# Experts of a mixture layer: the array's two column halves take two column sets of one 128-row piece, transposes turn, row halves scatter

## The reference, cut to what matters

```python
def moe_ffn(h, w_router, b_router, w_gu, b_gu, w_down, b_down):
    logits = h @ w_router + b_router
    top_logit, top_idx = lax.top_k(logits, 4)        # 4 of 32 experts
    top_p = softmax(top_logit)
    ...
    def expert_block(tok, p, e):                     # tok: the tokens of expert e
        gu = h_pad[tok] @ w_gu[e] + b_gu[e]          # 1024 -> 2048
        glu = minimum(gu[:, :1024], 7.0)
        lin = clip(gu[:, 1024:], -7.0, 7.0)
        act = glu * sigmoid(1.702 * glu) * (lin + 1.0)
        return (act @ w_down[e] + b_down[e]) * p     # 1024 -> 1024
    # the results are summed per token
```

## Time and profile before

| | us |
|---|---|
| median of 3 runs | 2990.94 (2989.73 to 2991.04) |
| the profiled execution's own time | 2974.59 |
| its span, first to last instruction | 2972.8 |
| PE busy | 2789.9 (94%) |
| DVE busy | 1296.0 (44%) |
| ACT busy | 950.0 (32%) |
| first unit on PE / last one issued | 1034.88 / 2015.69 + 8.59 |

### The profile page before, as it was taken

The page is one execution under the profiler, slowest core; times in us unless marked ns, Lnnn a source line. Parts: engine busy times, 40 slices in busy tenths (PEclk is TensorE's granted clock), DMA queues, the critical chain, the costliest instruction groups (busy, mean ns, idle before and its releaser), DMA issues. The chain is left out here.

```text
span 2972.8 us, 42557 instructions
## 1 busy us (share of the span) xinstructions
PE 2789.9 (94%) x17128; PEld 2054.6 (69%) x17129; DVE 1296.0 (44%) x2776; ACT 950.0 (32%) x1893; POOL 151.9 (5%) x175
## 2 busy tenths in 40 slices
PE   7899999979989899999999999997977999978998
PEld 3799989846779744444444444445956999966998
DVE  3456666657745501111011110104754666563665
ACT  2355555412215211111111111113432445332453
POOL 0232233100000000000000000000000000000000
PEclk9899999989969999999999999998956999975999
DMA  6331110055116699999999999984410556420563
GB/s 202 59 72 29 32 41 15 1 173 179 48 43 186 222 409 409 409 409 409 409 409 409 409 409 409 409 358 148 132 39 19 164 175 182 127 68 8 173 184 119
DMA packets 257679, 602.46 MB, mean 203 GB/s; under 512 B 26082, under 2 KB 82633, under 8 KB 257353
## 3 DMA queue, kind: packets, MB, share of 16 engines
q1 hardware_dynamic: 256396, 599.25, 56.5%
q10 hardware_dynamic: 1085, 0.45, 0.1%
HBM read 595.24 MB, written 4.39 MB: 202 GB/s over the span
## 5 line engine op out<-in xcount | busy, mean ns | idle before, releaser
L2828 PE MATMUL banks<-xs_r,w_hi 128*128 128x272 f32 (+1 forms) x1632 | 474.7, 291 | 29.1 <-DVE w_raw_r L3250 20.2
L2832 PE MATMUL banks<-xs_r,w_raw_r 128*128 128x272 f32 (+1 forms) x1632 | 472.2, 289 | 0.0
L2829 PE MATMUL banks<-xs_r,w_hi 128*128 128x272 f32 (+1 forms) x1632 | 469.7, 288 | 0.0
L2420 PE MATMUL banks<-moe_raw,moe_xs 128*64 128x512 f32 x2048 | 465.9, 597 | 1.1 <-ACT gu_tok L2524 1.1
L2367 DVE TENSOR_TENSOR gu<-banks,vec 128x512 f32<-128x512 f32 x64 | 44.3, 692 | 673.2 <-PE banks L2448 673.2
L3072 ACT ACTIVATE w_hi<-w_raw 128x512 fp32r<-128x512 f32 (+1 forms) x416 | 257.4, 620 | 245.2 <-PE banks L2832 201.5
L2828 PEld LDWEIGHTS banks<-xs_r,w_hi 128*128 128x128 f32 x1632 | 310.8, 190 | 34.2 <-issue 26.3
L2832 PEld LDWEIGHTS banks<-xs_r,w_raw_r 128*128 128x128 f32 x1632 | 310.7, 190 | 2.9
L2829 PEld LDWEIGHTS banks<-xs_r,w_hi 128*128 128x128 f32 x1632 | 311.2, 191 | 0.2
L2420 PEld LDWEIGHTS banks<-moe_raw,moe_xs 128*64 128x64 f32 x2048 | 138.6, 137 | 249.5 <-issue 239.7
L3250 DVE TENSOR_TENSOR w_raw_r<-w_raw,w_hi 128x512 fp32r<-128x512 f32 (+1 forms) x416 | 271.8, 677 | 55.9 <-ACT w_hi L3072 51.9
(11 more groups left out here) (482 smaller groups left out, 4450.3 us busy)
## 6 DMA issues: line engine op xcount, KB each, us to landing
moe_raw<-in_w_gu SPq DMA_DIRECT2D x256, 1024.0 KB, 18.5
moe_raw<-in_w_down SPq DMA_DIRECT2D x128, 1024.0 KB, 18.5
w_raw<-in_w_ff SPq DMA_DIRECT2D x256, 256.0 KB, 3.0
w_raw<-in_w_in SPq DMA_DIRECT2D x112, 256.0 KB, 2.7
gdn_w<-in_w_in SPq DMA_DIRECT2D x32, 512.0 KB, 4.0
mod_ring<-in_w_mod SPq DMA_DIRECT2D x16, 1024.0 KB, 5.5
ring_mod<-in_w_mod SPq DMA_DIRECT2D x4, 2048.0 KB, 20.2
wh<-in_w_in SPq DMA_DIRECT2D x8, 1024.0 KB, 9.5
```

The costliest lines, as they stand in the source:

```text
L2420: ins = pe.matmul(ps[pair(e) + c][k * SLOTS:(k + 1) * SLOTS, :], x[:, 2 * q + k, :], raw[n % UNITS][:, k * D + c * 512:k * D + c * 512 + 5 ...
L2828: pe.matmul(bank, w_hi, x[:, 0, 0:n_cols], start=first, stop=False)
L2829: pe.matmul(bank, w_hi, x[:, 1, 0:n_cols], start=False, stop=False)
L2832: ins = pe.matmul(bank, w_lo, x[:, 0, 0:n_cols], start=False, stop=last)
```

## The change

In `unit` both column halves of the array now hold the same 128-row piece k (the loops over k and c change places), and half c takes its own 512 of the 1024 columns. The sum over all 1024 features is then complete within one partition half. For `d`, half c has columns 512c to 512c+511; for `g` and `u` the columns are dealt in blocks of 128, even blocks to half 0 and odd ones to half 1, which makes the streamed operand four pieces of 128 with a step of 256. A g, u or d result needs one bank instead of two: g and d in bank pair(e), u in pair(e)+1. Two waits of TensorE on `gu_out` ahead of the u units go away, and the d units wait for the first `t_free` only. `out` and `results` copy 512 columns. `turn` is 4 full transposes in place of 8 matmuls. `scatter` has 4 matmuls that sum over 64 partitions, row half c with columns c; t is now the outer loop, and the two counts that `last_act` and `last_dve` wait for follow.

```diff
-                    act.wait_ge(scat, NEXP + 2 * c)
+                    act.wait_ge(scat, NEXP + c)
...
-                    dve.wait_ge(scat, NEXP + 2 * c + 1)
+                    dve.wait_ge(scat, NEXP + 2 + c)
...
-                    for c in range(2):
-                        for k in range(2):
-                            ins = pe.matmul(ps[pair(e) + c][k * SLOTS:(k + 1) * SLOTS, :], x[:, 2 * q + k, :],
-                                            raw[n % UNITS][:, k * D + c * 512:k * D + c * 512 + 512], start=(q == 0), stop=(q == 3))
+                    for k in range(2):
+                        w = raw[n % UNITS][:, k * D:(k + 1) * D]
+                        for c in range(2):
+                            out = ps[pair(e) + (ph == "u")][c * SLOTS:(c + 1) * SLOTS, :]
+                            ins = pe.matmul(out if ph == "d" else out.rearrange("p (j x) -> p j x", x=P), x[:, 2 * q + k, :],
+                                            w[:, c * 512:(c + 1) * 512] if ph == "d" else
+                                            w.rearrange("p (j c x) -> p c j x", c=2, x=P)[:, c],
+                                            start=(q == 0 and k == 0), stop=(q == 3 and k == 1))
...
-                    for i in range(8):
-                        s, m = i // 4, i % 4
-                        ins = pe.matmul(ps[pair(e) + h][:, i * SLOTS:(i + 1) * SLOTS], gs[:, s, (4 * h + m) * P:(4 * h + m + 1) * P],
-                                        fold, start=True, stop=True)
+                    for i in range(4):
+                        s, j = i // 2, 2 * h + i % 2
+                        ins = pe.transpose(ps[pair(e) + h][:, i * P:(i + 1) * P], gs[:, s, j * P:(j + 1) * P], ident)
...
-                        t, c = i % 2, i // 2
-                        ins = pe.matmul(ps[4 + 2 * t + c][:, :], pickTs[e % 2][:, t * P:(t + 1) * P], y[:, c * 512:(c + 1) * 512],
+                        t, c = i // 2, i % 2
+                        rows = slice(c * SLOTS, (c + 1) * SLOTS)
+                        ins = pe.matmul(ps[4 + 2 * t + c][:, :], pickTs[e % 2][rows, t * P:(t + 1) * P], y[rows, 0:512],
                                         start=False, stop=(e == NEXP - 1))
...
-                pe.wait_ge(gu_out, 1)
...
-                    pe.wait_ge(t_free, 2 * e + 2)
+                    pe.wait_ge(t_free, 2 * e + 1)
...
-                        pe.wait_ge(gu_out, 2 * e + 3)
...
-                    act.activation(gs[:, (ph == "u") * 1, :].rearrange("p (b n) -> p b n", b=2),
-                                   ps.all[:, pair(e):pair(e) + 2, :], ACT.Copy).then_inc(gu_out, 1)
+                    act.activation(gs[:, (ph == "u") * 1, 0:512], ps[pair(e) + (ph == "u")][:, :], ACT.Copy).then_inc(gu_out, 1)
...
-                    act.activation(y.rearrange("p (b n) -> p b n", b=2), ps.all[:, pair(e):pair(e) + 2, :], ACT.Copy,
-                                   scale=gslots[e % 2][:, 0:1]).then_inc(y_out, 1)
+                    act.activation(y[:, 0:512], ps[pair(e)][:, :], ACT.Copy, scale=gslots[e % 2][:, 0:1]).then_inc(y_out, 1)
```

## The result

The changed kernel takes 2961.66 us (median of 4 runs, 2954.71 to 2967.06); the kernel before, run beside it, 2990.85. The ratio is 0.9902, with an interval of 0.988 to 0.9924: faster by 29.2 us, where 19.7 were forecast. The time is 3.8 us under the low end of the forecast's range. The profiled execution of the changed kernel has a span of 2958.1 us. Three of all the timed executions, of 3033, 7534 and 9863 us, are in no figure here.

A forecast was written before the change was run, and what follows sets the result against it. TensorE and the weight stream were both taken as full, TensorE lagging 23.3 us, with the stream bounding after the change. The last round's terms gave a 19.7 us gain: 2990.94 - 19.7 = 2971.2 us, range 2965.5 to 2979.

The forecast's parts named there:

- The bound and the ceiling: Expert stage: stream already at its own ceiling, 409 GB/s; after the change TensorE waits for loads, some 3.8 us a round.
- rival (a): Weight stream is not at its ceiling and speeds up when units are released sooner: time 2870 to 2965; chance 0.04.
- The stream's end: End of the experts' weight loads: nothing moves the stream, so it still ends near 2001.0.
- When the lag is gone: TensorE's 23 us lag behind the stream is used up after six or seven of 31 rounds, ten at the upper bound.
- The round: TensorE's work for one expert falls from 30.94 to 27.0 us, bounds 26.7 and 28.3, under the stream's 30.8.
- rival (c): The split streamed operand of g and u runs slower; at a factor of 2, about 3300 us; chance 0.05.
- The turn: Four transposes at 0.12 us make 0.48 instead of 1.93, saving 1.45 per turn, 2.9 per round.
- The scatter: Row halves overlap as column halves do: 2.5 us instead of 3.51, saving 1.0 a round; bounds 2.15 to 3.75.
- The changes of shape: Changing the array's shape around the scatter costs some 0.15 us each, 0.3 in the scatter's 2.5.
- The end: Last round, laid out from the stream's end at 2001.0: L2212 at 2010.15 instead of 2029.89, gain 19.7 us.
- Rival (d): The gain comes but part is lost in the last round to clock and drains: 8 to 12 us; chance 0.07.
- rival (b): No change: the timed runs' extra 16.35 us lie in the stream; gain 3 to 6, time 2985 to 2988; chance 0.06.

The follow-up runs named there:

- Early units: Six weight units loaded ahead of the expert stage: changed kernel's stage 1007.9 us, median 2957.8 (0.9893); kernel before's stage 1040.1 us, median 2990.01 (0.9995).
- lengthened turns: Changed kernel with each turn's four transposes done four or eight times over: stage 1019.4 and 1099.2 us, medians 2964.51 (0.9911) and 3045.41 (1.0186).
- the last run: Changed kernel with half of each d unit not loaded and all four scatter matmuls in one row half: stage 959.9 us, median 2908.69 (0.9737).
- third execution of the changed kernel: Profiled execution from the second repeat of the changed kernel, unchanged: span 2956.0 us, stage 1019.9; that repeat's median 2962.42 (0.9925).
- theory B: Claim tested by repeating both kernels unchanged: longer executions have a slower weight stream. Kernel before ran 22.5 us longer, 1.6 of them in the stage; medians 2984.63 and 2964.59.

## Why the prediction was right in the stage and wrong in the total

**The bound and the ceiling** were right. The stream kept 409 GB/s and 1.03, and rival (a) is out. Early units and lengthened turns confirm on both sides that it is the limit.

The stream's end, forecast at 2001.0 and 7.5 later in this execution, came at 2009.

**When the lag is gone**: forecast after six or seven rounds, in fact after four. The first wait for a load comes at 1157, 144 us into the stage. 23.3 / 3.8 had the lag vanish evenly, but the eight units at a round's end take 13.9 us where the stream needs 20.6 for them, so within a round TensorE gets 6.7 us ahead of its mean and meets the stream there first. It cost nothing.

**The round**: forecast 27.0, measured 26.84. The units are unchanged (5.30, 1.87), so rival (c) is out: the split operand of 4 x 128 runs at the plain one's speed. The turn is 0.58 and not 0.48: a turn of 16 MATMULs takes 1.89 and one of 32 takes 3.64 in the two runs with lengthened turns, so a transpose is 0.11 and the step to other work 0.14, which the mean of 0.12 over sixteen had hidden. The scatter is 1.91, below even the lower bound of 2.15. That bound counted five steps of 0.43, the first and the last MATMUL alone. The weight loads at that place come as four at once and then twos every 0.43, four steps in all. The changes of shape, put at 0.3 inside the scatter, show only in part there, 1.91 being four steps and 0.2; the neighbours have the rest, 0.07 more in the slots and 0.11 in the fetch. With turns at +0.2, the scatter at -0.6 and the neighbours at +0.2 the forecast's 27.0 becomes the 26.84; the terms were off in both directions. The overlap itself, taken over from column halves, was the right choice, and the shared half of the last run is what its opposite would have looked like. The drain that the Trainium skill's "TensorEngine Tiling (Array Packing)", Key Properties, warns of is at most these 0.4 us here, both changes together.

**The end**, with all forecast times moved by the 7.5 us by which this execution's stage started later: ACT's copy 2001.6 forecast, 2002.40 measured; to the add 1.25 and 1.34; to L2212 from there, 2017.6 forecast and 2016.88 measured. Terms in it were off against each other. The last four d units take 7.12 to ACT's copy and not 8.64: the clock, feared to fall, stayed at 1.00 through them. The prediction read a clock of 1.00 "through the whole stage" from rows that end at 2002. Its 8.64 has another clock in it, as this stretch of the kernel before shows (0.66 granted):

```profile
2010.00:2020.00 10.00, 9.22 (x46) 6.15 (x47) 3.22 (x8) 0.83 (x2) 0.00 (x0) 0.66 0.01 2
```

Against that, ACT's copy came 0.8 later than laid out from the stream's end. Of the lag's 23.3 us some 4 are left at the end: the last unit is done at 2005.78 + 7.09 = 2012.87, the stream at 2009. From there to L2212 it is 4.0 us where it was 5.6. The stage was forecast to lose 19.7 us and lost 20.8, so the match is closer than its terms were. Rival (d) is out as the account of the result, but its mechanism is real: in the third execution of the changed kernel the clock fell in these four units and cost 1.7 us (8.78 against 7.09).

**The total** is where the prediction failed, in one step: "The profiled execution lies 16.35 us under the median of the runs; I take that as lying outside the stage". Outside the stage it does lie, as the forecast chose against rival (b), which falls with theory B. But the step also treated it as a constant offset that the changed kernel's median would have again. What is constant between an execution's own time and its span is 1.8 us (2959.89 and 2958.1; 2974.59 and 2972.8). The other 14.5 us were this one execution's luck: its rest, 1934.3, was at the short end of 1933.7 to 1955.2. What the runs showed in the constant's place is a rest that moves by 21 us. The difference of two medians is then not the stage's gain alone, but that plus whatever the two samples' rests differ by. For the medians of the first comparison the rest is 2990.85 - 1.8 - 1039.2 = 1949.9 and 2961.66 - 1.8 - 1018.4 = 1941.5; so 20.8 of the 29.2 us are the stage and 8.4 are the rest.

The range had the same fault. It was made of the stage's terms alone, 2965.5 to 2979.0, and held nothing for the rest, though the three runs of before agreed within 1.3 us while the profiled one stood 16 under them: a spread that was visible at the time and should have widened it by several us on both sides. The repetitions say how much. The kernel before against itself moved by 5.2 us (2984.63 against 2989.85), and the changed kernel gave 0.9902, 0.9911 and 0.9925; the forecast's own ratio is 2971.2 / 2990.94 = 0.9934, outside the first two intervals and inside the third.

**Does a part of the 8.4 us belong to the change?** The single timed executions can tell: all but those of the kernel before in the first comparison are on record with their span and mean granted clock. What the mean clock lacks to 1.00, times two and times the span, is the time at half clock. The 77 executions of the kernel before and the 20 of the changed one lie on two nearly parallel lines in it, with 0.36 us for each us at half clock. At equal time at half clock the changed kernel is **21.1 us** shorter, with an interval of 20.5 to 21.7. That is the stage's 20.8 once more, from other executions. The plain means, 2987.2 and 2963.0, differ by 24.2, and the 3 us more go with a mean clock of 0.9309 against 0.9300. So beyond the stage's 21 us nothing is left for work that the change saved, and the 8.4 us of the first comparison are what a few executions of each kernel can differ by.

**What stays open** is why the clock fell for longer in one execution than in another, and whether the change has a small part in that. The rests of the profiled executions overlap, but the stretches behind the stage do not, 926.6 to 927.2 for the changed kernel and 928.2 to 934.2 for the one before; with three of each, and 933.2 in two variants of the changed kernel, that shows nothing. Where both kernels were repeated side by side, their medians lie 20.0 and 24.2 us apart. No run here sets the clock outside the stage, so that the clock causes the spread is not shown; the two only go together.

## To carry to other kernels

Where two resources are both full, ask for the lag at which one follows the other: it is the whole gain that the follower can have, and a shortened stream beside a lengthened piece of the follower's work measures both limits in two runs. Forecast a change in one stage from that stage's length, and put the stage on the rest's typical length with its spread, not on one profiled execution and an offset. Once a stage is bound by a stream, its start and its buffers are what is left to gain.

## What the runs showed of the hardware

- Matmuls of 64 rows in the two row halves run beside each other in any program order: 8 MATMULs of 512 columns in 1.91 to 1.93 us whether the halves alternate or come two by two, and in 3.62 with all in one half.
- The granted clock stayed at 1.00 from 1040 to 2020 in the first profiled execution of the changed kernel, with TensorE busy nine tenths of the time and with gaps of 0.6 to 0.7 us between units. In the third it fell to half for 3.4 us at 2002, in the last four units, behind gaps of 0.70 and 1.63 us that the first has as well.
- Around a scatter in row halves, between matmuls of the full array, a round pays at most 0.4 us: 0.2 in the scatter itself over its four steps of 0.43, 0.07 before it and 0.11 in the fetch behind it.
- Code that was not touched, ahead of the stage, took 1004.9 to 1021.0 us from one execution to the next, with the clock at half for 113 to 150 us of it: 0.43 us for each. Over the whole program it was 0.36 us for each us at half clock, in 97 executions.
- The stream ends raggedly: its share was full to 2001, 0.80 from 2001 to 2002, a mean of 0.37 from 2003 to 2010, and nothing from 2009 on. Some of the sixteen engines being done before others would give that; the share is their mean and doesn't show them one by one.
